# Forward sweep of a bidirectional scan: which exponent is used is chosen by a predicated copy in PSUM, and the rear direction's diagonal moves into the coefficient of the values

## What is computed

```python
def ssd_chunked(xs, dt, a, bm, cm, h0):            # CHUNK = 128, 16 heads of 64, 2 groups, state 128
    acs = jnp.cumsum((dt * a).reshape(b, nc, CHUNK, g, r), axis=2)
    seg = acs[:, :, :, None] - acs[:, :, None, :]
    decay = jnp.exp(jnp.where(lower, seg, -jnp.inf))
    cb = jnp.einsum('bctgn,bcsgn->bctsg', cc, bc)
    y_diag = jnp.einsum('bctsgr,bcsgrp->bctgrp', cb[..., None] * decay, xdt)
    ...                                            # states carried from chunk to chunk, y_off from them
    return (y_diag + y_off).reshape(b, l, h, p), s_final

y_f, s_f = ssd_chunked(xs, dt[:, :, 0], a[0], bm, cm, h0_f)
y_b, s_b = ssd_chunked(rev(xs), rev(dt[:, :, 1]), a[1], rev(bm), rev(cm), h0_b)
y = y_f + rev(y_b) + d_skip[:, None] * xs
```

## Time and profile before

| | us |
|---|---|
| median of 3 runs (lowest, highest) | 2822.95 (2816.64, 2823.3) |
| the profiled execution, its own time | 2829.5 |
| its span | 2827.7 |
| PE busy, share of the span | 2672.9 (95%) |
| DVE busy | 1658.7 (59%) |
| ACT busy | 608.1 (22%) |
| POOL busy | 988.0 (35%) |

### The profile page before, as it was taken

One profiled execution on the slowest core, in us unless ns is written; L12 is line 12 of the kernel. 1 busy time (PEld: TensorE's weight loads), 2 busy tenths in 40 slices (PEclk: granted clock), 3 DMA queues, 4 the chain that ended last, 5 costly groups with the idle time before them and its releaser, 6 DMA issues. The chain is left out here.

```text
span 2827.7 us, 32173 instructions
## 1 busy us (share of the span) xinstructions
PE 2672.9 (95%) x12390; PEld 2146.4 (76%) x12390; DVE 1658.7 (59%) x2219; ACT 608.1 (22%) x871; POOL 988.0 (35%) x515
## 2 busy tenths in 40 slices
PE   8889999999999999987888999989989999999997
PEld 5778777778888888866775776578767888888885
DVE  6887555756556665676747986953475222222247
ACT  4222242311110011133232104632131110001111
POOL 2122225554333343541212432012645333333353
PEclk9999999999999999998999999999989999999998
DMA  3111132223222332221001343241322111111122
GB/s 139 39 51 45 51 142 82 97 82 98 97 89 91 102 96 96 97 101 61 31 30 38 112 127 112 99 177 45 116 93 90 53 45 47 50 52 45 52 69 102
DMA packets 88484, 228.88 MB, mean 81 GB/s; under 512 B 27520, under 2 KB 30720, under 8 KB 88384
## 3 DMA queue, kind: packets, MB, share of 16 engines
q1 hardware_dynamic: 52384, 172.81, 18.3%
q10 hardware_dynamic: 36000, 54.69, 6.1%
HBM read 197.98 MB, written 28.31 MB: 80 GB/s over the span
## 5 line engine op out<-in xcount | busy, mean ns | idle before, releaser
L215 POOL CAST w_hi<-w_raw 128x1024 fp32r<-128x1024 f32 x254 | 289.0, 1138 | 1774.6 <-PE ps L228 1755.8
L224 PE MATMUL ps<-a_hi,w_hi 128*128 128x512 f32 x2080 | 694.7, 402 | 47.3 <-PEq L2942 14.5
L217 POOL TENSOR_TENSOR w_lo<-w_raw,w_hi 128x1024 fp32r<-128x1024 f32 x254 | 696.0, 2740 | 20.3
L226 PE MATMUL ps<-a_lo,w_hi 128*128 128x512 f32 x2080 | 677.9, 393 | 0.0
L228 PE MATMUL ps<-a_hi,w_lo 128*128 128x512 f32 x2080 | 676.7, 393 | 0.0
L224 PEld LDWEIGHTS ps<-a_hi,w_hi 128*128 128x128 f32 x2080 | 391.4, 191 | 151.0 <-issue 58.3
L226 PEld LDWEIGHTS ps<-a_lo,w_hi 128*128 128x128 f32 x2080 | 396.1, 190 | 83.3
L228 PEld LDWEIGHTS ps<-a_hi,w_lo 128*128 128x128 f32 x2080 | 395.3, 190 | 84.3
L226 PE MATMUL ps<-g_b,w_hi 128*128 128x512 f32 x1216 | 412.6, 391 | 0.0
L224 PE MATMUL ps<-g_b,w_hi 128*128 128x512 f32 x1088 | 364.4, 392 | 11.2 <-DVE g_b L1806 11.2
L228 PE MATMUL ps<-g_b,w_lo 128*128 128x512 f32 x1088 | 362.1, 390 | 0.0
(11 more groups left out here) (459 smaller groups left out, 2682.2 us busy)
## 6 DMA issues: line engine op xcount, KB each, us to landing
w_raw<-in_wstream SPq DMA_DIRECT2D x254, 512.0 KB, 3.5
ada_w<-in_ada_w ACTq DMA_DIRECT2D x25, 512.0 KB, 3.5
ada_w_b<-in_ada_w ACTq DMA_DIRECT2D x25, 512.0 KB, 3.5
y_by_token<-y ACTq DMA_DIRECT2D x12, 512.0 KB, 3.3
x_res_b<-in_xT SPq DMA_DIRECT2D x2, 2048.0 KB, 11.2
x_block<-x_res_b SPq DMA_DIRECT2D x16, 256.0 KB, 3.0
z_rows<-ada_w ACTq DMA_DIRECT2D x8, 512.0 KB, 2.9
u_rows<-pad ACTq DMA_DIRECT2D x8, 512.0 KB, 4.2
```

What stands on the lines that cost most here:

```text
L215: pool.tensor_copy(k.w_hi[:, s, :], k.w_raw[:, s, :]).then_inc(k.w_high, 1)
L217: pool.tensor_tensor(k.w_lo[:, s, :], k.w_raw[:, s, :], k.w_hi[:, s, :].bitcast(F32), ALU.subtract).then_inc(k.w_split, 1)
L224: pe.matmul(o, w_hi, a_hi[:, c], start=first, stop=False)
L226: pe.matmul(o, w_hi, a_lo[:, c], start=False, stop=False)
```

## The change

In the forward sweep the masks and their identity matmuls go. `exponents(i, g)` computes for one group both directions, forward into banks 0 and 1 and rear into banks 2 and 3, with four matmuls 64 rows deep in alternating row halves. DVE's `choose(i, g)` then overwrites, in PSUM, the forward exponents by the rear ones where s > t (the old forward mask's bits serve as the predicate). One exponential per group is left, no sum of decays, and the weights are made in place in `big`, which now holds two chunks. `exponents` of the next chunk is split around `st`, the own part around the next chunk's `products_cb`.

Since a single exponent now stands at each place, the diagonal holds the forward decay alone. The rear direction's part there (dt_rear times the diagonal of C times B) is added to the skip coefficient: a table `own` of 8 chunks x 16 heads, made in `phase4` and used in the backward sweep where `head_rows` was used.

```diff
 # open_scan, phase4
-    v.consts, v.square = sb("scan_consts", [P, SCAN_COLS]), sb("scan_square", [P, 3, P], F32R)
+    v.consts = sb("scan_consts", [P, SCAN_COLS])
+    v.own = sb("own_weight", [P, NC, SSM_HEADS])
+        own_bc = [[(0, NC, v.x_rows[:, :])],
+                  [(0, 3, k.ada_w[:, KT * P - 3 * P:KT * P]), (3, 5, wdt_raw), (5, 7, dta...), (7, NC, v.own...)]]
 # PE, behind the last gemm of phase4
+            pe.wait_ge(k.pair_free[1], XBC_END // 2)
+            pe.wait_ge(s["own_in"], len(own_bc[0]) + len(own_bc[1]))
+            for g in range(NGRP):
+                for c0, c1, home in own_bc[g]:
+                    for c in range(c0, c1):
+                        ins = pe.matmul(own_sums[:, g * NC + c:g * NC + c + 1], home[:, (c - c0) * P:(c - c0 + 1) * P],
+                                        k.mean_col[:, :], start=True, stop=True)
+            ins.then_inc(s["own_out"], 1)
             pe.wait_ge(s["sums_ready"], 1)
-            pe.wait_ge(k.pair_free[1], XBC_END // 2)
 # DVE, phase4
             first_tiles(3)
+            dve.wait_ge(s["silu"], 2 * XS0)
+            for g in range(NGRP):
+                for c0, c1, home in own_bc[g]:
+                    tt(home, v.bc[:, g, c0 * P:c1 * P], v.bc[:, NGRP + g, c0 * P:c1 * P], ALU.mult).then_inc(s["own_in"], 1)
             with dve.Fori(0, PAIRS) as j:
...
-            dve.tensor_copy(v.square[:, 0, :], k.mats[:, IDENT, :])...
-            dve.tensor_copy(v.square[:, 1:3, :], v.consts[:, 0:2 * P]...)...
+            dve.wait_ge(s["own_out"], 1)
+            for g in range(NGRP):
+                ch.link(tt(v.own[:, :, hs], dt[:, 0:NC, rear], bc(own_sums[:, g * NC:(g + 1) * NC], 2, HPG), ALU.mult))
+            ch.link(stt(out=v.own[:, :, :], in0=v.own[:, :, :], scalar=1.0 * D_MODEL,
+                        in1=bc(v.rows[:, 64:64 + SSM_HEADS], 1, NC), op0=ALU.mult, op1=ALU.add))
 # PE, phase5
-            def exponents(i):
+            def exponents(i, g):
                 pe.wait_ge(s["moving_ready"], i + 1)
-                for j in range(EXPS):
...
+                if i or g:
+                    pe.wait_ge(s["e_ready"], NGRP * i + g)
+                if i and g == 0:
+                    pe.wait_ge(s["cb_ready"], i)
+                for b in range(2):
+                    at = g * HPG + b * HPG // 2
+                    for r in range(2):
+                        rows = slice(r * P // 2, (r + 1) * P // 2)
+                        ins = pe.matmul(k.ps[:, 2 * r + b, :]..., v.l_rows[rows, here(i)],
+                                        moving[rows, at:at + HPG // 2, :], start=True, stop=True)
+                ins.then_inc(s["d_done"], 1)
             def products_cb(i):
-                pe.wait_ge(s["e_ready"], EXPS * i + 3)
+                pe.wait_ge(s["chosen"], NGRP * (i + 1))
 # ACT, phase5
             def exps(i):
...
+                if i >= 2:
+                    act.wait_ge(s["diag_done"], i - 1)
+                for g in range(NGRP):
+                    act.wait_ge(s["chosen"], NGRP * i + g + 1)
+                    act.activation(big[:, i % 2 * NGRP + g, :], pair[0], ACT.Exp).then_inc(s["e_ready"], 1)
 # DVE, phase5
-                ch.link(tt(heads(y_even[:, :]), values(c), bc(v.rows[:, 64:64 + SSM_HEADS], 2, HDIM), ALU.mult))
+                ch.link(tt(heads(y_even[:, :]), values(c), bc(v.own[:, c, :], 2, HDIM), ALU.mult))
-            def add_decays(i):
...
+            def choose(i, g):
+                dve.wait_ge(s["d_done"], NGRP * i + g + 1)
+                fore, rear = (p.rearrange("p (h t) -> p h t", h=HPG) for p in pair)
+                dve.copy_predicated(fore, bc(after, 1, HPG), rear).then_inc(s["chosen"], 1)
```

More of the change, by code:

```diff
@@ L2376, in phase5 @@
         BWD_JOBS = 2
-        EXPS = 2 * NGRP
-        ident_r, masks = v.square[:, 0, :], [v.square[:, 1 + r, :] for r in range(2)]
+        after = v.consts[:, SC_FORE:SC_FORE + P].bitcast(I32)
         back = 2 * CC
@@ L2453, in here @@
                 return slice(i * P, (i + 1) * P)
-            def exponents(i):
+            def exponents(i, g):
                 pe.wait_ge(s["moving_ready"], i + 1)
-                for j in range(EXPS):
[L2459 to L2467, removed]
-                    for b, out in enumerate(outs):
-                        at = g * HPG + b * HPG // 2
-                        ins = pe.matmul(out, v.l_rows[rows, here(i)], moving[rows, at:at + HPG // 2, :], start=False, stop=True)
-                    ins.then_inc(s["d_done"], 1)
+                if i or g:
[6 more added lines that the diff above has]
+                        rows = slice(r * P // 2, (r + 1) * P // 2)
+                        ins = pe.matmul(k.ps[:, 2 * r + b, :].rearrange("p (h t) -> p h t", t=P), v.l_rows[rows, here(i)],
+                                        moving[rows, at:at + HPG // 2, :], start=True, stop=True)
+                ins.then_inc(s["d_done"], 1)
@@ L2485, in forward @@
                 ins.then_inc(s["off_done"], 1)
+                if i + 1 < NC:
+                    exponents(i + 1, 0)
                 pe.wait_ge(s["xw_ready"], back + NC + i + 1)
@@ L2492, in forward @@
                 if i + 1 < NC:
-                    exponents(i + 1)
+                    exponents(i + 1, 1)
+                pe.wait_ge(s["fore_ready"], i + 1)
+                own_chunk(i, 0)
+                if i + 1 < NC:
                     products_cb(i + 1)
-                pe.wait_ge(s["fore_ready"], i + 1)
[L2496 to L2499, removed]
-                    ins = pe.matmul(Xf[y_at][:, h * HDIM:(h + 1) * HDIM], weights[g][:, cols],
-                                    v.tok[:, i, VAL + h * HDIM:VAL + (h + 1) * HDIM], start=True, stop=True)
-                ins.then_inc(s["diag_done"], 1)
+                own_chunk(i, 1).then_inc(s["diag_done"], 1)
             for q in range(2):
                 pe.wait_ge(k.pair_free[q], UZ_END // 2)
-            exponents(0)
+            for g in range(NGRP):
+                exponents(0, g)
             products_cb(0)
@@ L2561, in exps @@
             def exps(i):
[L2562 to L2569 removed]
+                if i >= 2:
+                    act.wait_ge(s["diag_done"], i - 1)
+                else:
+                    act.wait_ge(s["pooled"], KT)
+                for g in range(NGRP):
+                    act.wait_ge(s["chosen"], NGRP * i + g + 1)
+                    act.activation(big[:, i % 2 * NGRP + g, :], pair[0], ACT.Exp).then_inc(s["e_ready"], 1)
             def copy_cb(i):
```

61 lines of the change are left out of this document (33 added, 28 removed).

## The result

| | before | with the change |
|---|---|---|
| median, 4 runs each (lowest, highest) | 2821.79 (2816.64, 2823.3) | 2836.51 (2829.23, 2840.76) |
| ratio | 1 | 1.0047, 95% interval 1.0027 to 1.0068 |
| the profiled execution, its span | 2829.5, 2827.7 | 2829.23, 2827.4 |
| sums of the convolution to the first state addition | 215.5 | 218.4 |
| backward sweep | 205.8 | 205.8 |

What follows compares the result with a forecast made beforehand. The forward sweep looked PE-bound with DVE close behind; after the change a serial ACT and DVE loop sets it. -1.9 sweep, +4.9 clock, +1.0 and +0.4 phase4 gave +4.4 us, 2827.4 against the median 2822.95; range 2817 to 2842.

Steps and rivals of the forecast that it cites:

- the clock's term: Forward sweep: PE's waits sometimes bring 3.4 us at half speed, 1.4 us at every second chunk boundary: +4.9, between 0 and 9.8.
- serial halves: Rival, exponent batches: row halves don't run side by side, a batch costs 1.32 us; +6, 2833.5; chance 0.10.
- The loop, 13.93 us a period: Forward sweep: serial chain through DVE and ACT, from one chunk's first predicated copy to the next, 13.93 us against 13.47 before.
- a copy in two passes: Rival, DVE in the forward sweep: the predicated copy takes two passes, 17 us more, 2844.5 with the clock; chance 0.13.
- My reason for the halves (alternation): Exponent batch on PE: alternating halves and banks, as in matmuls elsewhere, lets two run side by side, so 0.66 us.
- The fast end of the copy: Predicated copy on DVE: a fast end 0.7 below 1.22 us, excluded for its PSUM access and predicate; 1.14 was taken.
- The first rival, DVE as the bound: Forward sweep: a chunk costs only DVE's 11 or 10 operations, -10.6 + 1.4, 2813.8; chance 0.07.
- The sweep's start, 11.89 us: Forward sweep up to chunk 1's first copy: batches, copies, exponentials and `moving`, 11.89 us.
- The tail, 17.12: Forward sweep's end: nine DVE operations, `st`, own part, hand-overs and last sum, 17.12 us.
- my sum without the clock: Whole forward sweep, from its start, periods and tail at full clock: 110.09 us, against 111.94 before.
- phase4, +1.4: `phase4`: products of C and B uncovered before the convolution, +1.0, and one-column products at the stage's end, +0.4.
- -1.9: Whole forward sweep without the clock: 110.09 us against 111.94, a gain of 1.9 us.

Runs made afterwards that it cites:

- e2: The change with `off` and `st` of chunks 1 to 6 each done twice on PE, against the kernel before: ratio 1.0032, forward sweep 117.48 us.
- e5: The change with each batch's four exponent matmuls ordered both of one row half first, then both of the other: one run, 2837.84; forward sweep 121.04 us.
- e1: The change with ACT making `a_hi` before the 16 `moving` copies, against the kernel before: ratio 1.0018, forward sweep 109.62 us.
- e11: The kernel before with `a_hi` ahead of the `moving` copies and 12 idle ACT copies before `moving` of chunks 2 to 7: one run, 2859.51.
- e9: The change with `a_hi` first, `phase4` products behind the first convolution pair, `off` of chunks 1 to 6 done twice, against the kernel before: ratio 0.9991.
- e0: The change again, unaltered, against the kernel before: ratio 1.0048, forward sweep 124.48 us.
- e3: The change without the diagonal's own part (no products of C and B, no `own` table), against the kernel before: ratio 1.0055.
- e7: The change with `a_hi` first, `moving` split by group, and `phase4` products behind the first convolution pair, against the kernel before: ratio 1.0017.
- e6: The change with `a_hi` first and `moving` split by group, eight copies between the two exponentials, against the kernel before: ratio 1.0023.

## Why the prediction was right, and where it wasn't

The measured time, 2836.51, lies in the range (2817 to 2842), and the forecast's account names the two places of the loss; but its middle, +4.4, is a third of the 13.3, and 0.47% is beyond the 0.3% within which I had put most of the chance (0.57 against 0.36 for slower). It also lies above the ends that I gave the clock's term, 2822.5 to 2832.3. The range holds it only because I had stretched it for serial halves with a bad clock, and the halves weren't serial: that the number is inside is in part luck.

- *The loop, 13.93 us a period.* Right: 14.00 in the change's one period without low clock, 13.98 to 14.00 in e2. The terms hold one by one: batch 0.66, copy 1.13 from start to start, DVE waiting 1.3 to 1.5 us for `a_hi`. The rivals of a copy in two passes and of serial halves fall with them. My reason for the halves (alternation) was not needed, by e5. The fast end of the copy was misread: plain copies of 128x1024 in the trace before take 0.69 us, which is 0.5 below 1.22 and not 0.7; nothing was added up from it.
- *The first rival, DVE as the bound.* It was wrong for the change and right one edit away: e1's 12.59. What held it off was what I had named, `a_hi` behind `moving`.
- *The sweep's start, 11.89 us.* It took 14.22. The term left out 1.28 us for ACT's table load, which the old order hid and which the wait for the first copy uncovers. Of the other 1.05 about 0.9 is the clock's: the second batch and C times B take 1.22 us each there instead of 0.73 and 0.66, and 0.50 and 0.36 of that are on the path.
- *The tail, 17.12.* 17.28.
- *The clock, +4.9 (0 to 9.8).* This is the step that failed in size: "a wait of this size sometimes costs a stretch of 3.4 us at half speed", priced at 1.4 us for every second boundary. What the sweep took over my sum without the clock is 122.53 - 110.09 = 12.44 us; less the table load, 11.2 are left. Some 10.3 of them are the clock's: 0.9 at the start, 77.4 - 5 x 14.0 = 7.4 in the five periods, and 13.63 - 11.65 = 2.0 in the one without `a_hi`, which at full clock takes 11.65 in e5; the other 0.9 are small misses of the sum. Even the upper end of the term, 9.8, is below that. The stretches were 3.4 to 13.7 us long, not 3.4, and lay over the sweep's start and five of its seven boundaries. I had priced a stretch by the work that happened to stand behind the wait and capped it at one unit of those two rows, though those came behind single waits, and a loop repeats its waits. Measured, a microsecond at 0.50 in this sweep costs 10.3/51.2 = 0.20 us. The mechanism itself is shown: PE's waits in the old kernel bring it (e11), and more work on PE takes it away (e2, e9). The Trainium skill's rule that the throttled level is the default and activity releases it (TensorE: Matmul & The Clock Gate, What's actually happening) agrees with the direction of all three. That PE can be busy throughout and stay at 0.50 for 20.3 us (e11) doesn't agree with it.
- *phase4, +1.4.* It is +2.9, and +2.7 to +3.1 by e0 and e3. The 0.9 at the convolution (forecast 1.0, by a slip: 1391.30 + 2.5 is 1393.8, so 0.9) and 3.52 - 2.98 = 0.54 at the one-column products (0.4) are as worked out. The 1.4 to 1.5 us left over I had not priced. Of it 1.06 is again the clock: PE's longer wait is followed by 6.8 us at 0.50 instead of 3.4, and the same work takes 15.33 us instead of 14.27. The thirteen traces agree that the place of the products decides between the two lengths. The remaining 0.4 is not taken apart.

Summed again with what was measured: -1.9 + 1.3 + 10.3 + 0.9 + 2.9 = +13.5.

## What to carry to other kernels

Work removed from an engine that is on a loop's side, not in it, becomes waiting; first draw the loop, and move what doesn't belong to it (here one copy, `a_hi`) out of the way, which gave back more of the sweep in the trace (12.9 us) than the change had cost it (10.6), and in the old order 4.5 us, of which the program's median shows under 2. On PE, count the waits that a change creates as a cost of their own: in a loop they recur, and the granted clock may be down for as long as they do. Before a stage's gain is believed, read the next stage as well: in e7 it was lost there. When the first instruction of a kind on ACT gets a new wait in front of it, its table load gets it as well.

## What the hardware showed that I had not expected

- How long and how full PE's waits are doesn't tell alone whether the clock falls. In e1 it stayed at 1.00 for 34.1 us with PE busy for 24.99 of them and waits of 2.61 us every 12.6; in e6 it fell behind 6.6 us with 5.52 busy and a single wait of 1.08; in e9 waits of 0.90 and 0.66 a period never brought it down. The two loops differ in their period and in where the waits lie; why the one falls is open.
- A low stretch, once there, can outlast full work: PE was busy for 13.60 of 13.60 us in the change and for 20.30 of 20.30 in e11, at 0.50 throughout.
- A copy under a predicate, PSUM to PSUM with an int32 predicate from SBUF, costs DVE the same 1.22 us as an addition of 128x1024.
- In a batch of four 64-row matmuls, two on each half of the array, the starts come in pairs within 0.01 us also when the program issues two of the same half first (e5). Two alone on one half start 0.34 us apart (the kernel before).
- In e7 and e9 the 1.5 us gained in `phase4` came back as a low stretch at the start of the backward sweep, in code that wasn't touched. What brings it is open.
